# Depthwise convolution moved ahead of the main attention and shared by three engines, its LayerNorm moved inside the attention

## What is computed

```python
h = x + 0.5 * g1 * swiglu(modulate(x, g_ffn1, s1, sc1), w1_gate, w1_up, w1_down)
u, q, k, v, qi, ki, wi, g_c, g_a = split_in(modulate(h, g_mix, s2, sc2), w_in, ...)   # one projection
y = depthwise_conv(concat([prefix, u]), w_dw, 31 taps, 512 channels) + b_dw
conv_out = silu(layernorm(y, ln_g, ln_b)) @ w_conv_out
att = attend(q, k, v, qi, ki, wi).reshape(B, T, 512) @ w_attn_o     # top 256 keys by the indexer
h = h + g2 * ((sigmoid(g_c) * conv_out + sigmoid(g_a) * att) @ w_out)
h = h + 0.5 * g3 * swiglu(modulate(h, g_ffn2, s3, sc3), w2_gate, w2_up, w2_down)
y = rmsnorm(h, g_final)
```

## Time and profile before

| | us |
|---|---|
| runs: median (lowest, highest) | 2978.55 (2977.64, 2982.11) |
| the profiled execution's own time | 2990.24 |
| its span | 2988.4 |
| mean granted TensorE clock | 0.956 of full speed |
| busy: PE, DVE, ACT, POOL | 2751.2, 1558.8, 582.1, 861.7 |
| projection's end (last gate tile) | 1592 |
| main attention, first to last product | 1711 to 1894 |
| first mix product on VectorE | 1937.0 |

### The profile page before, as it was taken

One profiled execution on the slowest core, in us unless ns is written; L12 is line 12 of the kernel. 1 busy time (PEld: TensorE's weight loads), 2 busy tenths in 40 slices (PEclk: granted clock), 3 DMA queues, 4 the chain that ended last, 5 costly groups with the idle time before them and its releaser, 6 DMA issues.

```text
span 2988.4 us, 43550 instructions
## 1 busy us (share of the span) xinstructions
PE 2751.2 (92%) x16084; PEld 2462.6 (82%) x16084; DVE 1558.8 (52%) x2590; ACT 582.1 (19%) x1056; POOL 861.7 (29%) x458
## 2 busy tenths in 40 slices
PE   7999999999998889999995778788899999999996
PEld 3799999999996758888994235588799999999995
DVE  2434443334446559999999587553343333333335
ACT  1411111111112321121111246510130011100103
POOL 0322222222221226433221292022122322333220
PEclk9999999999999989999997869899899999999998
DMA  6322222222222413311225200133111111111101
GB/s 233 120 71 70 68 67 69 70 70 70 70 67 94 104 34 89 94 43 43 81 92 211 77 1 1 44 123 107 35 36 43 49 42 42 47 52 42 49 21 58
DMA packets 207446, 209.10 MB, mean 70 GB/s; under 512 B 13071, under 2 KB 160643, under 8 KB 206457
## 3 DMA queue, kind: packets, MB, share of 16 engines
q1 hardware_dynamic: 197180, 181.04, 19.2%
q10 hardware_dynamic: 10181, 26.90, 2.8%
HBM read 172.37 MB, written 28.94 MB: 67 GB/s over the span
## 4 chain that ended last, share of the span: by engine, by line
PE 68%; DVE 19%; issue 5%; ACT 3%; DMA 2%; SPq 1%; DVEq 1%; ACTq 0%; POOL 0%; POOLq 0%
PE main L245 19%; PE main L247 19%; PE main L246 19%; DVE top L1131 6%; DVE pick L1144 5%; PE aux L415 2%; PE main L1463 1%; PE main L334 1%; DVE pick L1118 1%; SPq L1296 1%; DVE conv_y L1206 1%; ACT tmp L455 1%; PE aux L1491 1%; PE main L1480 1%; PE aux L344 1%
## 5 line engine op out<-in xcount | busy, mean ns | idle before, releaser
L245 PE MATMUL main<-nhi,whi 128*128 128x352 f32 (+1 forms) x3288 | 1076.4, 327 | 29.9 <-DVE nlo L506 18.4
L247 PE MATMUL main<-nhi,wlo 128*128 128x352 f32 (+1 forms) x3288 | 1063.3, 323 | 0.0
L246 PE MATMUL main<-nlo,whi 128*128 128x352 f32 (+1 forms) x3288 | 1062.9, 323 | 0.0
L234 POOL CAST whi<-raw 128x1024 fp32r<-128x1024 f32 x189 | 200.6, 1061 | 1877.6 <-PE main L247 1453.9
L245 PEld LDWEIGHTS main<-nhi,whi 128*128 128x128 f32 (+1 forms) x3288 | 622.6, 189 | 56.9 <-issue 23.1
L246 PEld LDWEIGHTS main<-nlo,whi 128*128 128x128 f32 (+1 forms) x3288 | 624.4, 190 | 0.8
L247 PEld LDWEIGHTS main<-nhi,wlo 128*128 128x128 f32 (+1 forms) x3288 | 622.2, 189 | 0.7
L236 POOL TENSOR_TENSOR wlo<-raw,whi 128x1024 fp32r<-128x1024 f32 x189 | 475.6, 2516 | 15.2
L639 DVE TENSOR_TENSOR tmp<-main,tmp 128x352 f32<-128x352 f32 x132 | 69.2, 524 | 779.7 <-PE main L247 775.8
L660 DVE SCALAR_TENSOR_TENSOR h<-main,ada,h 128x352 f32<-128x352 f32 (+1 forms) x528 | 294.3, 567 | 95.0 <-PE main L247 94.8
L245 PE MATMUL main<-hid_hi,whi 128*128 128x352 f32 x1056 | 341.7, 324 | 0.3
(11 more groups left out here) (237 smaller groups left out, 2541.5 us busy)
## 6 DMA issues: line engine op xcount, KB each, us to landing
ada_raw<-in_w_ada SPq DMA_DIRECT2D x18, 2048.0 KB, 8.3
raw<-in_w_gate SPq DMA_DIRECT2D x44, 512.0 KB, 3.8
raw<-in_w_up SPq DMA_DIRECT2D x44, 512.0 KB, 3.8
raw<-in_w_down SPq DMA_DIRECT2D x44, 512.0 KB, 3.4
raw<-in_w_in SPq DMA_DIRECT2D x40, 512.0 KB, 3.9
gate_d<-zraw ACTq DMA_DIRECT2D x16, 528.0 KB, 2.7
gates<-gate_d SPq DMA_DIRECT2D x16, 528.0 KB, 4.9
zsw<-zraw ACTq DMA_DIRECT2D x50, 132.0 KB, 2.4
```

What stands on the lines that cost most here:

```text
L234: pool.tensor_copy(whi[:, slot], raw[:, slot]).then_inc(hi_done, 1)
L245: pe.matmul(bank, whi[:, slot, w], hi(c), start=(i == 0), stop=False)
L246: pe.matmul(bank, whi[:, slot, w], lo(c), start=False, stop=False)
L247: last = pe.matmul(bank, wlo[:, slot, w], hi(c), start=False, stop=(i == n - 1))
```

## The change

- **Chunk 0** moves from VectorE to ScalarE and GpSimd. ScalarE starts it at the first gate tile of the former loop (`conv_start`, an Identity with scale and bias), then makes one product of 128x1024 after every evacuation (`conv_product`); GpSimd adds it (`conv_add`) behind each split, three a tile. The loops over the gate tiles are unrolled for it. Products alternate between two buffers: product i waits for add i-2.
- **Chunk 3** goes the same way in the preparation, in halves of 128x512 (60 products, 60 adds). ScalarE makes 14 products after the first page copies, one ahead of each of the 18 copies of k and v, 4 after each later pair of pages, the rest ahead of the sample softmax.
- **Chunk 1** runs on VectorE where chunk 0 was, **chunk 2** where chunk 1 was. VectorE and GpSimd have no taps left in the attention.
- k is turned before v, v is loaded once chunk 0 is complete, and SyncE asks for value pages after all 18 groups rather than 9. VectorE waits for the v transfers before the attention.
- **The LayerNorm** is woven into the attention: sums at u = 3 to 5, mean at n = 8 to 12, squares at n = 9 to 13, their sums at u = 7 to 9, roots at n = 18, 19, 21, products at n = 19 to 23, Silu at n = 24, 26, 28. Its split in `conv_hi` and `conv_lo` goes to GpSimd.
- **The mix** multiplies the convolution's part first, then the attention's.

```diff
+            for L in range(NZ, NZ + 3):
                 for t in range(NTC):
+                    conv_add(pool, 0, 1 + NTC * (L - 3 - Z_LOOP) + t)
...
+            for L in range(Z_GATE, NZ):
...
+                    act.activation(zraw[:, s, tcs(t)], main[:, 3 * (L % 2) + t, 0:TC], ACT.Sigmoid).then_inc(z_free, 1)
...
+                    if (L, t) == (Z_LOOP, 0):
+                        conv_start(act, 0)
+                    conv_product(act, 0, 1 + NTC * (L - Z_LOOP) + t)
...
-            conv_chunk(dve, 0)
+            conv_chunk(dve, 1)
...
+        def conv_start(act, c):
+            act.activation(conv_y[:, c, 0:SEQ], uext[:, c, 0:SEQ], ACT.Identity, scale=taps[:, c, 0:1],
+                           bias=par[:, ROW_BDW + c:ROW_BDW + c + 1]).then_inc(cv_prod, 1)
...
+        def conv_product(act, c, i):
...
+            elif 0 <= i < 2 * (CW - 1):
+                k, half = 1 + i // 2, i % 2
+                act.wait_ge(cv_sum, SUM_0 + max(0, i - 1))
+                at = 512 * half
+                act.activation(prod_m2[:, half, :], uext[:, 3, k + at:k + at + 512], ACT.Copy,
+                               scale=taps[:, 3, k:k + 1]).then_inc(cv_prod, 1)
...
+        def conv_add(pool, c, i):
...
+                pool.wait_ge(cv_prod, PROD_0 + 1 + i + 1)
+                pool.wait_ge(cv_sum, SUM_0 + max(0, i - 1))
+                y = conv_y[:, 3, 512 * half:512 * half + 512]
+                pool.tensor_tensor(y, y, prod_m2[:, half, :], ALU.add).then_inc(cv_sum, 1)
...
-            sp.dma_start(vraw[:, :, :], v_d).then_inc(v_in, 16)
             sp.dma_start(ka[:, :, :], k_d).then_inc(k_in, 16)
             sp.dma_start(qa[:, :, :], q_d).then_inc(q_in, 16)
+            sp.wait_ge(cv_sum, SUM_0)
+            sp.dma_start(vraw[:, :, :], v_d).then_inc(v_in, 16)
...
-            sp.wait_ge(kv_t, 9)
+            sp.wait_ge(kv_t, 18)
...
+                if 3 <= u < 6:
+                    ln_mean(u - 3)
+                if 7 <= u < 10:
+                    ln_squares(u - 7)
...
-                for i, (xh, xl) in ((1, (o_hi, o_lo)), (0, (conv_hi, conv_lo))):
+                for i, (xh, xl) in ((0, (conv_hi, conv_lo)), (1, (o_hi, o_lo))):
...
+            act.wait_ge(cv_sum, SUM_0)
+            conv_start(act, 3)
             for b in range(2):
                 copy_pages(b)
+            conv_products(14)
             for g in range(18):
                 t = g % 9
                 n = P if t < 8 else NSAMP
+                conv_products(1)
                 act.wait_ge(kv_t, g + 1)
...
             for b in range(2, NSEQ):
                 copy_pages(b)
+                conv_products(4)
+            conv_products(2 * CW)
...
+                if n in (9, 11, 13):
+                    ln_square((n - 9) // 2)
+                if n in (18, 19, 21):
+                    ln_sqrt((18, 19, 21).index(n))
+                if n in (24, 26, 28):
+                    ln_swish((n - 24) // 2)
...
-            conv_chunk(dve, 1, 0, 18)
+            conv_chunk(dve, 2, 0, 18)
...
-            conv_chunk(dve, 1, 18)
+            conv_chunk(dve, 2, 18)
...
+            dve.wait_ge(v_out, 16 * 9)
...
-                for i in TAPS_AT[n]:
```

More of the change, by code:

```diff
@@ L1196, in conv_chunk @@
             with dve.Fori(max(k0, 1), k1) as k:
[L1197 to L1206 removed]
+                dve.wait_ge(cv, CV_DEC + CW * (c - 1) + k)
@@ new lines, in conv_add @@
+        def conv_add(pool, c, i):
+            if c == 0:
+                if not 1 <= i < CW:
+                    return
+                pool.wait_ge(cv_prod, i + 1)
+                if i > 1:
+                    pool.wait_ge(cv_sum, i - 1)
+                y = conv_y[:, 0, 0:SEQ]
+                pool.tensor_tensor(y, y, prod_m1[:, i % 2, 0:SEQ], ALU.add).then_inc(cv_sum, 1)
+            else:
+                half = i % 2
+                pool.wait_ge(cv_prod, PROD_0 + 1 + i + 1)
+                pool.wait_ge(cv_sum, SUM_0 + max(0, i - 1))
+                y = conv_y[:, 3, 512 * half:512 * half + 512]
+                pool.tensor_tensor(y, y, prod_m2[:, half, :], ALU.add).then_inc(cv_sum, 1)
@@ L1503, in turn_sums, with ln_mean, ln_squares @@
                 last.then_inc(ot_mm, 1)
+            def ln_mean(t):
+                if t == 0:
+                    pe.wait_ge(cv, CV_TOTAL)
+                    pe.wait_ge(cv_sum, SUM_ALL)
+                if t == 2:
+                    pe.wait_ge(ln_y, 1)
+                for c in range(4):
+                    last = pe.matmul(main[:, LN_BANK["mean"][t], 0:TC], ones[:, :], conv_y[:, c, tcs(t)],
+                                     start=(c == 0), stop=(c == 3))
+                last.then_inc(ln_s, 1)
+            def ln_squares(t):
+                pe.wait_ge(ln_sem["sq"], t + 1)
+                if t < 2:
+                    pe.wait_ge(ln_y, t + 2)
+                else:
+                    pe.wait_ge(ln_sem["sd"], 1)
+                for c in range(4):
+                    last = pe.matmul(main[:, LN_BANK["sq"][t], 0:TC], ones[:, :], sqc[:, c, tcs(t)],
+                                     start=(c == 0), stop=(c == 3))
+                last.then_inc(ln_sem["mm"], 1)
             logits(0)
             for u in range(NQ // 2 + 2):
+                if u + 1 == 16:
+                    pe.wait_ge(ln_sem["sd"], 3)
                 if u + 1 < NQ // 2:
                     logits(u + 1)
+                if 3 <= u < 6:
+                    ln_mean(u - 3)
+                if 7 <= u < 10:
+                    ln_squares(u - 7)
                 if u < NQ // 2:
@@ L1639, in turned, with ln_square, ln_sqrt, ln_swish @@
                         .then_inc(pt_e, 1)
+            def ln_square(t):
+                act.wait_ge(ln_y, t + 1)
+                act.activation(sqc[:, :, tcs(t)], conv_y[:, :, tcs(t)], ACT.Square).then_inc(ln_sem["sq"], 1)
+            def ln_sqrt(t):
+                act.wait_ge(ln_sem["mm"], t + 1)
+                if t == 2:
+                    act.wait_ge(ln_sem["ml"], 1)
+                act.activation(rstd_c[:, t % 2, :], main[:, LN_BANK["sq"][t], 0:TC], ACT.Sqrt, scale=1.0 / D_CONV,
+                               bias=eps).then_inc(ln_sem["sd"], 1)
+            def ln_swish(t):
+                act.wait_ge(ln_sem["ml"], t + 1)
+                for c in range(4):
+                    last = act.activation(conv_y[:, c, tcs(t)], conv_y[:, c, tcs(t)], ACT.Silu,
+                                          scale=par[:, ROW_LNG + c:ROW_LNG + c + 1],
+                                          bias=par[:, ROW_LNB + c:ROW_LNB + c + 1])
+                last.then_inc(ln_sem["af"], 1)
             for n in range(NQ + 8):
@@ L1761, in m2_dve @@
                     dve.tensor_tensor(otok[:, :], aux[:, b % 2, :], otok[:, :], ALU.mult).then_inc(at_m, 1)
+                    if b == 7:
+                        dve.drain().then_inc(mix_free, 3)
                 if n % H == 0 and n > H:
```

180 lines of the change are left out of this document (68 added, 112 removed).

## The result

The changed kernel takes 2994.51 us (median of 5 runs, 2991.32 to 2997.06); the kernel before, run beside it, 2980.72 (5 runs, 2977.64 to 2984.67). The medians lie 13.8 us apart. The ratio is 1.0037, 95% interval 1.0021 to 1.0053, which is 11 us; the two differ by 3 us. By either the kernel is slower, and by more than the 0.2% that a measurement here can tell. I had forecast 3007.5, so the sign was right and the loss was less than half of the 29 us that I had summed up.

A forecast was written before the change was run, and what follows sets the result against it. TensorE was busy 92% of the span, but preparation, attention and tail mattered, with GpSimd's adds setting the preparation's pace. Preparation +58, attention +4, tail -33 gave +29 us on 2978.55, so 3007.5 us, range 2962 to 3035.

The forecast's parts named there:

- VectorE's decode part, +6: Before the preparation: short VectorE products wait for GpSimd's last adds and split, 6 us later, bounds 0 and 9.
- The gate tiles and the projection, 0: Chunk 0 beside gate tiles: products and adds just fit, two tiles of slack per split, TensorE's projection costs 0.
- The tail, -33: Behind the attention: first mix product about 10 us after the last value product instead of 43, gain 33 us.
- 78 + 50 + 5 = 133: Preparation: 60 adds 78 us, 39 VectorE taps 50, small copies 5, all excluding each other; last add at 1741.
- since VectorE's taps fill them: Preparation: GpSimd's waits for a product while ScalarE copies add nothing, because VectorE's taps fill them.
- None is a second cost, being inside the sum: Preparation: key copies, TensorE's transposes and SyncE's value pages queued behind waiting ScalarE add nothing to the sum.
- The attention, -25 + 20.5 + 8 = +4: Main attention: 25 us of maxima waits return; LayerNorm costs 20.5 on TensorE and 8 showing from ScalarE (bounds 0 and 33).
- Short adds: First rival, preparation: 512-wide adds pass between taps, preparation +28, sum -1, 2977.5 us; chance 0.15.
- The clock: Second rival, attention: TensorE granted 2.4 GHz throughout, 18 us less, with preparation at its lower bound; 2959.5 us; chance 0.13.
- the third rival: ScalarE bounds attention blocks 1 to 3: all 33 us show instead of 8, sum +54, 3032.5 us; chance 0.17.
- The two bounds of my own: Attention: the prediction is wrong if it starts before 1745 or is under 165 us long.
- likeliest case's own 2993 to 3022: Whole kernel: range of the main forecast, from add bounds of 1.21 and three more caught instructions; chance 0.50.

The follow-up runs named there:

- e1: The kernel before, unchanged, profiled a second time; 2985.55 us.
- f1: Changed kernel with the key pages of sequences 4 and 5 issued ahead of SyncE's wait for 18 groups; attention start 1755.1 us.
- e2: Changed kernel with chunk 3's 60 products and 60 adds left out; median 2970.3 us.
- e3: Changed kernel with VectorE's 30 running taps of chunk 2 left out; attention start moved by 2.8 us.
- g2: e2 with the value rows loaded and turned ahead of the key rows again; median 2954.4 us.
- h2: e5 with value rows first, no ScalarE products for chunk 3, and its 30 taps on VectorE in the attention, GpSimd idle; attention 152.9 us.
- e5: Changed kernel with the LayerNorm and Silu put back behind the attention; median 2990.6 us.
- g3: f1 with the first two roots together and the three Silu thirds together at turn 44; attention no shorter than with Silus grouped earlier.
- h1: e5 with value rows first and chunk 3's products and sums on GpSimd alone beside the attention; 0.65% faster than the kernel before.
- g1: Changed kernel with f1's early key pages and e3's omission of chunk 2's running taps together; median 2985.7 us.
- i1: h1 with chunk 3's first six running taps on VectorE ahead of the attention; median 2960.6 us.

## Why the prediction was right or wrong

**Direction and shape: right.** A longer preparation outweighs the short tail, and the attention changes little. VectorE's decode part, +6: +7.2. The gate tiles and the projection, 0: TensorE's last gate product comes 1.0 us later than in before and 1.7 later than in e1, which are 0.7 apart. The tail, -33: behind fell from 44.2 or 43.4 to 10.4, so -33 to -34.

**The failed step: the 133 us of "78 + 50 + 5 = 133"** in the preparation. It is 115.3, and by its own terms: the 60 adds 60 x 1.23 = 73.8 instead of 78; the taps 33 x 0.97 = 32 instead of 50, because a pair of tap and add takes 2.20 and not 2.58, and because 33 taps, not 39, met an add; the small copies nothing that shows instead of 5. That makes 105.8, which is also the busy time of the 60 adds. The other 9.5 are GpSimd's waits for a product, 4 x 0.35 beside the copies of v and 8.1 while ScalarE waits for turned pages. Of these I had said that they add nothing "since VectorE's taps fill them". Five taps did pass in the 8.1 us, and GpSimd lost them all the same. From the Exp table to the attention I had 31.7; it was 33.4. The start came at 1756.6, not 1770: +45.5 (from the first profile of before) or +49.8 (from e1) in place of +58. This is one of two mis-sized terms; the other is the attention, below.

**"None is a second cost, being inside the sum": right for this kernel, and by little.** f1 shows that SyncE's pages are inside it: issued earlier, they bring the start no more than 1.5 us forward. e2, e3 and g2 show that they are a limit of their own, 20 us above the old one, and take over as soon as the adds are gone. I had named the queue and not priced it.

**The attention, -25 + 20.5 + 8 = +4: both sides too small.** The departure of the taps and of GpSimd's work gave 41 (181.7 to 140.8), not 25, in two parts. TensorE's wait for the maxima fell from 32.9 us to 1.8, so that 31 came back and not the 25 that I took: hardly any of it was plain latency. And TensorE's own busy time fell by 10 (141.4 to 131.4) for the same products, at a mean granted clock of 0.89 in place of 0.83; this I had put at nothing, since a low clock is no wait. With 30 taps and GpSimd idle (h2) the wait is 15.7 us; the rest of it I put down to taps that GpSimd's instructions held up, which I knew from the earlier trace rows but had left out of this term. TensorE's waits in e5:

```profile
PE main L1494 <- DVE mx L1794: 1.8, 4, 0.9
```

The LayerNorm cost 34 to 36: 17.7 for the sums and 17 in longer waits, 13 of them for ScalarE, where I let 8 show. The sum was -6.6 and not +4, with two errors of 16 and 6 that partly cancel.

Together: against e1, +49.8 - 6.7 - 33 = +10.1 for the first mix product (1932.0 to 1942.1), and 8.9 for the span. Against the first profile of before, from which I had reckoned, it is +45.5 - 6.6 - 33.8 = +5.1; the medians say 11 to 14.

**The rivals.** Short adds don't pass between taps: a tap's record grows from 1.28 to 2.02. The clock: the granted clock reached the 2.4 GHz level at about 1770, 14 us into the attention, as the LayerNorm's first sums ended (1765.9 to 1770.4). Before, it first reached it some 37 us in and lay mostly there from some 72 on (0.97 after 1788). It was not held in the changed kernel either: from 1800 to 1840 the mean is 0.72. The preparation was not at its lower bound, so the clock did not decide. ScalarE did bound the attention's second quarter, half as much as the third rival said.

The Trainium skill (SBUF — State Buffer, "Who interferes with whom") has VectorE and GpSimd block each other for such operands. The trace agrees that they do, and puts a size on it: 2.20 us for a pair that takes 1.47 and 1.23 apart, so about half a microsecond of the pair still overlaps. The Trainium skill has a drain of 1.38 us with each table load (ScalarE: Activation LUTs, "What ACT_TABLE_LOAD costs"). It shows in no row: in g3 the Silus begin 0.01 us behind the load's end, and the load 0.02 behind the work ahead of it.

**The two bounds of my own.** The attention was not under 165 us and its start not before 1745, and 2994.5 is even inside the likeliest case's own 2993 to 3022. They were too wide to catch errors of 13 us in the start and 11 in the attention. Of the signs that I had named, the key copies near 1640 (1638), the twelve table loads and the 10 us behind the last value product came; the Exp table near 1738 (1723.2), adds 2.6 apart (2.20) and taps of 2.5 (2.02) did not.

## What to carry to other kernels

Work that goes to an idle engine is paid where its hand-overs stand in a busy one's queue: sixty products of 0.72 us made ScalarE wait for every add, and 30 of them were dear in both places tried, while the same sums made by GpSimd alone, with no one waiting, cost the attention 2 us (h1) and a wait of 7 behind it. Before filling an idle engine, look at which pairs exclude each other and put them in different stages: taps in the preparation, GpSimd in the attention. And where two queues end within a few microseconds of each other, removing one shows nothing; remove both, as g1 did, before calling either harmless.

## What was not expected of the hardware

GpSimd's product over 128x1024, one multiply with no tap beside it, takes 2.85 us (h1), longer than the add of two tensors, 2.35. With a multiply and an add in one instruction, and read from offset 0, it was 1.19. The trace of the kernel before has both, one behind the other, so the size could have been read there before h1 ran:

```profile
1696.93 1.19 POOL L1360 TENSOR_SCALAR conv_acc<-uext,taps,par 128x1024 f32<-128x1024 f32 x1 [100.71 <-DVE conv_y L1206]
1698.21 2.85 POOL L1364 TENSOR_SCALAR conv_tmp<-uext,taps 128x1024 f32<-128x1024 f32 x1
```

Which of the two differences matters was not tried.

With GpSimd busy and no taps, TensorE waited longer for VectorE's maxima, which read PSUM and one tensor in SBUF: 1.8 us in e5, 4.8 in h1 and 11.6 in i1, and the attention grew by 2 and 7 us. The maxima's own records are no longer (0.75 us on average in all three), and i1 has less of GpSimd's work than h1, so it is not shown that GpSimd's instructions delay them. TensorE's waits in h1 and in i1:

```profile
PE main L1500 <- DVE mx L1796: 4.8, 9, 0.9
```

```profile
PE main L1500 <- DVE mx L1802: 11.6, 13, 2.2
```
